# Two transformer-style blocks on one core: the last mixer's weights split ahead of time and kept in DRAM, scan tables later, constant products at the norms

## What is computed

```python
x = layer_norm(ALPHA * x + short_conv_mixer(x))     # a_w_in (2048 x 6144), a_w_out
x = layer_norm(ALPHA * x + conv_ffn(x))             # ffn_w_up (2048 x 11264), ffn_w_down (5632 x 2048)
x = layer_norm(ALPHA * x + diff_attention(x))       # kv_w_k, b_w_q, kv_w_v, b_w_o
x = layer_norm(ALPHA * x + conv_ffn(x))
h = x + ab_layer(rmsnorm(x))                        # dilated attention and gated linear attention
h = h + cd_layer(rmsnorm(h))                        # the last mixer
out = rmsnorm(h) * final_g

def cd_layer(h, w_in, ...):
    u, qd, fd, idd, gate = split(h @ w_in)          # cd_w_in, 2048 x 6144
    yc = s5_mixer(u, ...)                           # a complex diagonal scan over time, w_glu 1024 x 1024
    f = lower_bound + (1 - lower_bound) * sigmoid(fd)
    od = chunked_gated_linear_attention(silu(qd), 1 - f, idd, log(f))   # 8 heads ("hgrn")
    yd = head_rmsnorm(od)
    return (concat([yc, yd]) * silu(gate)) @ w_out  # cd_w_out
```

## Time and profile before

| | before |
|---|---|
| median of 3 runs | 3239.39 us (3235.76 to 3240.88) |
| the profiled execution | 3238.17 us |
| its span in the trace | 3236.9 us |
| PE busy | 3062.1 us (95%) |
| PE weight loads busy | 2603.8 us (80%) |
| DVE busy | 2151.3 us (66%) |
| ACT busy | 1527.1 us (47%) |
| transfers | 596.75 MB, 184 GB/s |
| mean granted clock of TensorE | 0.978 of full speed |

### The profile page before, as it was taken

The page is one execution under the profiler, slowest core; times in us unless marked ns, Lnnn a source line. Parts: engine busy times, 40 slices in busy tenths (PEclk is TensorE's granted clock), DMA queues, the critical chain, the costliest instruction groups (busy, mean ns, idle before and its releaser), DMA issues. The chain is left out here.

```text
span 3236.9 us, 57237 instructions
## 1 busy us (share of the span) xinstructions
PE 3062.1 (95%) x25845; PEld 2603.8 (80%) x25870; DVE 2151.3 (66%) x2204; ACT 1527.1 (47%) x1406; POOL 64.5 (2%) x112
## 2 busy tenths in 40 slices
PE   8999999999999999999999999998999899888786
PEld 7888788888888787588888888886687777657685
DVE  5555866666555666468687776545765557998785
ACT  4343655444433544745455554335544534324543
POOL 0000000000000000001200000000000001000000
PEclk9999999999999999999999999999999999899898
DMA  8665455565565454455766566553445445554331
GB/s 285 209 208 183 148 204 196 208 209 201 204 206 200 154 180 159 157 169 170 267 228 218 206 224 244 196 182 120 163 149 196 151 163 203 172 189 156 113 118 66
DMA packets 295476, 596.75 MB, mean 184 GB/s; under 512 B 11824, under 2 KB 16048, under 8 KB 295104
## 3 DMA queue, kind: packets, MB, share of 16 engines
q1 hardware_dynamic: 287616, 564.22, 51.1%
q0 software_dynamic: 7616, 28.87, 2.4%
HBM read 577.32 MB, written 15.73 MB: 183 GB/s over the span
## 5 line engine op out<-in xcount | busy, mean ns | idle before, releaser
L1464 DVE TENSOR_TENSOR WL<-WF,WH 128x2048 bf16<-128x2048 f32 x533 | 1206.8, 2285 | 692.6 <-ACT WH L974 692.4
L506 PE MATMUL PSG<-XH,WH 128*128 128x256 bf16 x5648 | 1552.4, 275 | 49.8 <-DVE XL L1569 24.1
L506 PE MATMUL PSG<-XL,WH 128*128 128x256 bf16 x5648 | 1551.7, 275 | 0.0
L506 PE MATMUL PSG<-XH,WL 128*128 128x256 bf16 x5648 | 1551.4, 275 | 0.0
L974 ACT ACTIVATE WH<-WF 128x2048 bf16<-128x2048 f32 x533 | 1000.2, 1899 | 617.2 <-PE PSG L506 381.5
L506 PE MATMUL PSG<-SCR,WH 128*128 128x256 bf16 x4480 | 738.5, 273 | 0.0
L506 PEld LDWEIGHTS PSG<-XH,WH 128*128 128x128 bf16 x5648 | 557.1, 99 | 132.0 <-issue 62.4
L506 PEld LDWEIGHTS PSG<-XL,WH 128*128 128x128 bf16 x5648 | 556.9, 99 | 70.7 <-issue 0.8
L506 PEld LDWEIGHTS PSG<-XH,WL 128*128 128x128 bf16 x5648 | 556.8, 99 | 68.8
L506 PE MATMUL PSG<-SCR,WL 128*128 128x256 bf16 x2240 | 611.2, 273 | 0.0
L506 PEld LDWEIGHTS PSG<-SCR,WH 128*128 128x128 bf16 x4480 | 439.2, 98 | 55.8 <-issue 0.3
(11 more groups left out here) (240 smaller groups left out, 1554.2 us busy)
## 6 DMA issues: line engine op xcount, KB each, us to landing
WF<-ffn_w_up SPq DMA_DIRECT2D x176, 1024.0 KB, 5.8
WF<-ffn_w_down SPq DMA_DIRECT2D x88, 1024.0 KB, 5.1
WF<-ab_w_in SPq DMA_DIRECT2D x56, 1024.0 KB, 5.2
WF<-a_w_in SPq DMA_DIRECT2D x48, 1024.0 KB, 5.9
WF<-cd_w_in SPq DMA_DIRECT2D x48, 1024.0 KB, 5.2
WF<-a_w_out SPq DMA_DIRECT2D x16, 1024.0 KB, 5.2
WF<-kv_w_k SPq DMA_DIRECT2D x16, 1024.0 KB, 5.1
WF<-b_w_q SPq DMA_DIRECT2D x16, 1024.0 KB, 5.1
```

The lines of the kernel that those rows point to most:

```text
L506: return nc.tensor.matmul(o, lhsT, rhs, start=start, stop=stop, skip_group_check=True)
L1464: tt(l, w, h, ALU.subtract).then_inc(s_lo, 1)
```

## The change

**A plan of the ring.** A new function `ring_plan` writes one list of ring positions. The 68 chunks of the cd mixer (u and all that follow) are each split early: a position "keep" is inserted behind every fourth chunk of mix, up0, down0, kq, v and down1, and behind every twentieth of up1 (11, 22, 11, 8, 4, 8 and 4 positions). A "keep" chunk is loaded, split by ACT and DVE into the ring like any other, but no product uses it: SP stores the two halves (1 MB in all) to a DRAM tensor `kept_weights`. In the cd mixer SP loads each pair of halves from there straight into the ring, so that neither ACT nor DVE splits anything there. WH and WL become the two halves of one tensor WS, so that a pair is one transfer. The waits follow the plan: a ring position is free once TensorE is done with its chunk or, for a "keep", once its store has landed. The splits now look ahead by chunks that are multiplied (`split_ahead`), so that a "keep" between them is split too.

**Rates.** From the second cd_gate group to cd_out0 the side flows get four steps in a chunk's turn instead of three.

**Tables.** Both `idle` counts ahead of the 16 rounds of rotation tables grow by 14 steps.

**Constant products.** `fill(n)` puts n products of 128x256 bfloat16 of a constant matrix with itself behind the statistics of a norm on TensorE: 40 at each of the four layer norms, 32 behind the last statistics of the first block and 32 behind ab_out. Nobody reads their result.

```diff
+def ring_plan(groups, stage, count):
+    def span(name):
+        a, b = stage[name][0], stage[name][-1]
+        return groups[a]["first"], groups[b]["first"] + len(groups[b]["rows"])
+    first_kept = span("u")[0]
+    after = set()
+    for name, step, at in (("mix", 4, 6), ("up0", 4, 2), ("down0", 4, 2), ("kq", 4, 2), ("v", 4, 2),
+                           ("up1", 20, 10), ("down1", 4, 2)):
+        a, b = span(name)
+        after |= set(range(a + at, b - 1, step))
+    after = sorted(after)[:count - first_kept]
+    plan = []
+    for i in range(count):
+        plan.append(("kept" if i >= first_kept else "mul", i))
+        if i in after:
+            plan.append(("keep", after.index(i)))
+    assert len(after) == count - first_kept
+    return plan, first_kept
 def two_block_model(nc, A, out):
...
         WF = sb("WF", [128, RF, 4, 512])
-        WH = sb("WH", [128, RB, 4, 512], BF16)
-        WL = sb("WL", [128, RB, 4, 512], BF16)
+        WS = sb("WS", [128, RB, 2, 4, 512], BF16)
+        WH, WL = WS[:, :, 0, :, :], WS[:, :, 1, :, :]
         CN = sb("CN", [128, NCONST])
...
         groups, stage, chunks = weight_groups(A)
+        plan, first_kept = ring_plan(groups, stage, len(chunks))
+        KEPT = nc.dram_tensor("kept_weights", (len(chunks) - first_kept, 128, 2 * 2048), BF16).ap()
+        place = {n: p for p, (kind, n) in enumerate(plan) if kind != "keep"}
+        raw = [p for p, (kind, _) in enumerate(plan) if kind != "kept"]
+        raw_number = {p: n for n, p in enumerate(raw)}
+        def chunk_at(p):
+            kind, n = plan[p]
+            return chunks[n + first_kept if kind == "keep" else n]
+        def released(p):
+            kind, n = plan[p]
+            return (d_kept[n % 2], 16 * (n // 2 + 1)) if kind == "keep" else (s_mm, n + 1)
+        def split_done(p):
+            if plan[p][0] == "kept":
+                return d_ws[p % RB], 16 * len([q for q in range(p % RB, p + 1, RB) if plan[q][0] == "kept"])
+            return s_lo, raw_number[p] + 1
+        def split_ahead(i):
+            return place[min(i + LA, len(chunks) - 1)]
...
         def sync_program():
-            def load(i):
-                g, k0, rows = chunks[i]
+            def load(p):
+                if plan[p][0] == "kept":
+                    k = plan[p][1] - first_kept
+                    nc.sync.wait_ge(d_kept[k % 2], 16 * (k // 2 + 1))
+                    nc.sync.wait_ge(*released(p - RB))
+                    nc.sync.dma_start(WS[:, p % RB].rearrange("p h t n -> p (h t n)"), KEPT[k]).then_inc(
+                        d_ws[p % RB], 16)
+                    return
+                i = raw_number[p]
+                g, k0, rows = chunk_at(p)
                 src = g["w"][k0:k0 + rows, g["col"]:g["col"] + g["width"]].rearrange("(t p) n -> p t n", p=128)
...
                 nc.sync.dma_start(shaped(WF, i % RF, rows, g["width"]), src).then_inc(d_w[i % RF], 16)
+                if i >= RF and plan[raw[i - RF]][0] == "keep":
+                    q = raw[i - RF]
+                    k = plan[q][1]
+                    nc.sync.dma_start(KEPT[k], WS[:, q % RB].rearrange("p h t n -> p (h t n)")).then_inc(
+                        d_kept[k % 2], 16)
...
             nc.sync.dma_start(POSI, A["positions"].partition_broadcast(128)).then_inc(d_pos, 16)
-            for i in range(RF, len(chunks)):
-                load(i)
+            for p in range(RF, len(plan)):
+                load(p)
             for g in range(4):
...
+            FILL = ONE_D[:, :].bitcast(BF16)
+            def fill(n):
+                free(3)
+                for _ in range(n):
+                    mm(PB[:, 3, 0:T], FILL[:, 0:128], FILL, True, True)
             def sum_features(n, bank, first, last):
...
                 sum_tiles(1, SQ[1][:, 2:4, :], False, True).then_inc(s_tile, 1)
+                fill(40)
...
                 sum_tiles(1, SQF[g % 2], g == 0, g == 3).then_inc(s_tile, 1)
+            fill(32)
...
             side.drain()
+            fill(32)
...
             flags.add("idd")
-            for gi in stage["cd_gate"][0:3]:
-                gemm(gi, xh, xl, rate=3)
+            for n, gi in enumerate(stage["cd_gate"][0:3]):
+                gemm(gi, xh, xl, rate=4 if n else 3)
             side.until(s5_flow)
             for n, gi in enumerate(stage["glu"]):
-                gemm(gi, uh, ul, [(s_ul, k // 4 + 1) for k in range(8)] if n == 0 else None, rate=3)
+                gemm(gi, uh, ul, [(s_ul, k // 4 + 1) for k in range(8)] if n == 0 else None, rate=4)
             gated_0 = side.add_first(gated((0,)))
-            gemm(stage["cd_gate"][3], xh, xl, rate=3)
+            gemm(stage["cd_gate"][3], xh, xl, rate=4)
             gated_1 = side.add_first(gated((1,)))
             gated_h = side.add(gated((2, 3)))
-            residual("cd_out0", None, uh, ul, [(s_gl, 5 + k // 4) for k in range(8)], rate=3,
+            residual("cd_out0", None, uh, ul, [(s_gl, 5 + k // 4) for k in range(8)], rate=4,
                      before=lambda c: side.until(gated_0, *((gated_1,) if c else ())))
...
             def hi(i):
-                g, _, rows = chunks[i]
+                p = raw[i]
+                g, _, rows = chunk_at(p)
                 nc.scalar.wait_ge(d_w[i % RF], 16 * (i // RF + 1))
-                if i >= RB:
-                    nc.scalar.wait_ge(s_mm, i - RB + 1)
-                act(shaped(WH, i % RB, rows, g["width"]), shaped(WF, i % RF, rows, g["width"]),
+                if p >= RB:
+                    nc.scalar.wait_ge(*released(p - RB))
+                act(shaped(WH, p % RB, rows, g["width"]), shaped(WF, i % RF, rows, g["width"]),
                     ACT.Copy).then_inc(s_hi, 1)
-            def hi_to(i):
-                while state["hi"] <= min(i, len(chunks) - 1):
+            def hi_to(p):
+                while state["hi"] < len(raw) and raw[state["hi"]] <= p:
                     hi(state["hi"])
...
                 for c in range(len(g["rows"])):
-                    hi_to(g["first"] + c + LA)
+                    hi_to(split_ahead(g["first"] + c))
                     if before:
...
                 act(cs, tmp2, ACT.Sin, bias=cn("halfpi"), scale=-1.0).then_inc(s_tab, 1)
-                yield from idle(11)
+                yield from idle(25)
                 for n in range(16):
...
             def lo(i):
-                g, _, rows = chunks[i]
-                w, h, l = (shaped(t, i % n, rows, g["width"]) for t, n in ((WF, RF), (WH, RB), (WL, RB)))
+                p = raw[i]
+                g, _, rows = chunk_at(p)
+                w = shaped(WF, i % RF, rows, g["width"])
+                h, l = (shaped(t, p % RB, rows, g["width"]) for t in (WH, WL))
                 nc.vector.wait_ge(s_hi, i + 1)
...
-            def lo_to(i):
-                while state["lo"] <= min(i, len(chunks) - 1):
+            def lo_to(p):
+                while state["lo"] < len(raw) and raw[state["lo"]] <= p:
                     lo(state["lo"])
...
                 for c in range(len(g["rows"])):
-                    lo_to(g["first"] + c + LA)
+                    lo_to(split_ahead(g["first"] + c))
                     if before:
...
                 nc.vector.wait_ge(s_cp, 1)
-                yield from idle(9)
+                yield from idle(23)
                 for n in range(16):
```

24 lines of the change are left out of this document (13 added, 11 removed).

## The result

| | before | after |
|---|---|---|
| median of 4 runs each | 3240.14 us | 3317.0 us (3313.42 to 3323.41) |
| ratio | | 1.0243 (95% interval 1.022 to 1.0266) |
| span of the profiled execution | 3236.9 us | 3322.1 us |
| mean granted clock | 0.978 | 0.974 |
| transfers | 596.75 MB | 739.42 MB |

The forecast was 3205 us with a range of 3150 to 3240, so the time lies far outside, on the other side of before, where the third rival had it (3320 us, chance 0.08).

What follows compares the result with a forecast made beforehand. DVE was taken to bound the scan, the chain DVE, ACT, PE the heads, TensorE the rest. 3238.2-50-22-10-4-3+51+3+3 = 3206 us, stated as 3205, range 3150 to 3240.

Steps and rivals of the forecast that it cites:

- third rival: In up0, a store holds the queue longer than a load, each round 7.9 us too long: 3320 us; chance 0.08.
- the early splits in up0: Up0: fifth chunk lands at B+14.5 (B: ACT begins its splits after a group's results), 51 us added.
- The stages said to be free: Mix and down: early splits cost TensorE nothing where ACT and DVE wait for it.
- attention: Kq and v: twelve more splits of 4.2 us in flows with their own slack, 3 us added, bounds 0 and 15.
- The cd mixer: Last mixer, to the end of the kernel: 82 us saved in the forecast by stretch.
- Scan stretch: Cd mixer, scan beside 31 chunks: without splits TensorE sets the pace, 212 us instead of 262, 50 saved.
- Heads: Cd mixer, heads of hgrn beside 21 chunks: 171 us instead of 193, 22 saved, bounds 38 and 0.
- The end: End of cd mixer: at four steps a chunk the heads' flow fits beside the chunks, 10 us saved, bounds 13 and 0.
- second rival: Cd mixer heads are bound by their chain's length, so rate 4 only makes TensorE arrive sooner: 3233 us; chance 0.15.
- Tables: Rotation tables 14 steps later: ACT's 11.3 us wait for a transfer goes, 4 us saved.
- Constant products: Behind the norms at six places: clock stays at its upper level, 3 us saved in all, bounds 0 and 10.
- first rival: In up0, the store doesn't delay the load behind it, so up0 costs nothing: 3154 us; chance 0.25.

Runs made afterwards that it cites:

- small_store: The changed kernel, with each store and read-back of a kept pair moving only 64 KB instead of 1 MB: 3193.67 us (ratio 0.9871).
- store_on_act_queue: The changed kernel, with its stores issued by ACT on another queue at about the same moment: 3285.28 us (ratio 1.0166).
- store_one_later: The changed kernel, with each store issued behind one more load, that of the round's fifth chunk: 3232.11 us (ratio 0.9987).
- store_later: The changed kernel, with each store issued behind two more loads in SP's queue: 3199.25 us (ratio 0.9885).

## Why the prediction was wrong

**The step that failed** is the term of the early splits in up0: "So the fifth lands at 9.3 + 2 x 2.6 = B+14.5", and with it "The fourth is loaded at B+4.2 and lands at B+9.3 as before". It priced the store as one more megabyte in a row at 400 GB/s ahead of one load. The runs show a store beside two loads: in the changed kernel the fourth chunk lands 1.2 us late and the fifth 4 us later than without the store (B+16.4 in the mean; B+12.7 and B+12.3 in `small_store`), not 2.6. Besides, the prediction let slack carry three of the 22 groups without cost; the first round of up0 takes 23.9 us already and the second 26.3. The rest of that step holds. The prediction's round ends 9.2 us behind the landing of the fifth chunk (14.5 to 23.7), and in every kernel it does, within 0.7 us:

| kernel | fifth lands, two rounds | + 9.2 | from L1221 to L1221 |
|---|---|---|---|
| changed | B+16.9, 15.9 | 25.6 | 25.3, 25.5 |
| store_on_act_queue | B+15.0 | 24.2 | 24.6 |
| store_one_later | B+13.8, 14.3 | 23.2 | 23.4, 22.6 |
| store_later | B+12.3, 12.0 | 21.4 | 20.7, 21.6 |

Over all 21 rounds of up0 the means, in the order of the table, are 16.5, 15.3, 14.2 and 12.3 us for the landing and 25.4, 24.2, 23.1 and 21.3 us for the round, and `small_store` has 12.7 and 21.6. So some 0.3 to 0.6 us a round are the fifth split's own, and the rest of the 4.4 us are the store's. 22 groups at 25.4 instead of 21.0 us make 97 of the 102 us. The low clock there (0.94) was not foreseen, but since the loop of ACT and DVE sets the round, it needs no share of its own.

**The stages said to be free.** Of the 117 us between forecast and profile 51 are the stretch of up0, and 13 the cd mixer. Another 12 are mix, which "cost TensorE nothing where ACT and DVE wait for it", and 21 up1 and down1, where no cost was forecast. `store_later` takes them back, so they are the same store, which I had weighed in one stage only. 19 are attention, priced at 3 with a bound of 15: 18 of them stay with the store out of the way and go with its own early splits.

**The cd mixer** gives 69 us of the forecast 82, and the sum hides two errors. Scan stretch: 50 forecast, 49 measured to the first head; a round was to take 12.7 us and takes 13.0. Heads: 16 to 18.5 us were forecast for each, and 18.5 it is, from 25.2, which gives 40 us up to the seventh; but the prediction's stretch of heads ended with the last halves of hgrn's result, and from the first head to there it is 192 us before and 164 after, 28 gained where 22 were forecast. The end: "10 saved" was the step that failed. TensorE's wait of 6.6 us is gone as forecast, and still the end takes 72 us instead of 65, 7 lost, since I made the flow's steps fit beside fewer chunks and did not ask which products would then be left without a flow: 494 products stand there instead of 398. At rate 3 the end takes 66 us with 398 products, as before, so it never held a gain. The second rival (the rates only make TensorE arrive sooner) was right on what the rates bring in all, and wrong on the heads: they gain 30 us from the absent splits alone.

**Tables** 3 us of 4. **Constant products** nothing of 3: the half clock behind a norm was real, and TensorE still waits for the next piece at its full clock, as that step itself had said.

**The rivals.** The third had the right time with half of its mechanism, and so by luck. It said that the store costs more than a load, with the fifth chunk at B+19.7 and 166 us in up0; it was B+16.4 and 102 us, and the rest came from stages that it left out. The bound "slower once the store takes 2 us more than a load" was right in kind: store and load took 8.7 and 6.4 us. The evidence for it was in the earlier trace rows, 6.2 against 3.6 us for POOL's half megabyte, and 0.08 was too little for the one row in which a store had been measured. The first rival, at 3154 us, is what `small_store` nearly builds; it misses by 40 us, since attention, up0's own splits and the longer end remain.

## What to carry to other kernels

Work that is moved beside an idle engine brings transfers with it, and these land beside transfers that have a due time. Before placing such a store, find for each load of the loop how long the loop can wait for it, and issue the store where the next two loads to land have slack: here two places further in the same queue were worth 118 us, another queue at the same moment 32. A mean transfer rate over a stage doesn't show whether there is room in those few microseconds. When a loop's length depends on one landing, write it as landing plus remainder, and look for the landing in all stages in which the pattern recurs.
